# The keys of a paged cache brought in by blocks of 32 keys into all 128 partitions instead of by 256-column slices into 32 partitions

## The reference, cut to what matters

```python
def diff_attn_cached(q, k, v, kp, vp, lam):
    s_p = jnp.einsum('bqhd,bkhd->bhqk', q, kp).astype(F32) * scale
    s_n = jnp.einsum('bqhd,bkhd->bhqk', q, k).astype(F32) * scale
    ...
    a = _diff_combine(jnp.concatenate([s_p, s_n], axis=-1), lam)   # softmax, then map 0 - lam * map 1
    return (jnp.einsum('bhqk,bkhe->bqhe', a[..., :P], vp.astype(F32))
            + jnp.einsum('bhqk,bkhe->bqhe', a[..., P:], v.astype(F32)))

kp = cache_k[o][page_table].reshape(Bs, past, 2 * H_C, HD_C)       # cache_k (1, 320, 128, 16, 64)
vp = cache_v[o][page_table].reshape(Bs, past, H_C, 2 * HD_C)
```

## Time and profile before

| | |
|---|---|
| median of 3 runs | 2929.31 us (2927.39 to 2933.23) |
| the profiled execution's own time | 2932.32 us |
| its span, from the first to the last instruction | 2930.7 us |
| mean granted TensorE clock | 0.899 |
| TensorE, VectorE, ScalarE, GpSimd busy | 81%, 52%, 23%, 19% of the span |
| first key DMA issued, last key page turned | 1727.0 us, 2773.2 us |
| moved by DMAs in all | 536.70 MB |

### The profile page before, as it was taken

How to read it: one execution, slowest core, us unless ns; L and a number is a source line. 1 busy time by engine, 2 the same in 40 slices (tenths; PEclk the granted TensorE clock), 3 DMA queues, 4 the chain that set the end, 5 groups by cost and what they waited for, 6 DMA issues and landing times.

```text
span 2930.7 us, 44854 instructions
## 1 busy us (share of the span) xinstructions
PE 2387.4 (81%) x15136; PEld 1789.1 (61%) x15136; DVE 1523.6 (52%) x2401; ACT 670.7 (23%) x1767; POOL 543.7 (19%) x487
## 2 busy tenths in 40 slices
PE   8999999999859997999999983666657565656668
PEld 6889888988747774787888871322323232323347
DVE  5565643233246665324344326666667666657643
ACT  4122211111123333223111122222222122222221
POOL 4332432234000000002223200211111111111121
PEclk9999999999969999999999997878777777777779
DMA  5223322232177889223343349999999999999963
GB/s 168 80 81 102 104 84 78 80 118 81 65 188 235 272 273 298 89 86 104 94 127 92 110 130 254 294 282 288 289 276 289 263 267 277 280 267 274 276 196 115
DMA packets 443172, 536.70 MB, mean 183 GB/s; under 512 B 41365, under 2 KB 385314, under 8 KB 439754
## 3 DMA queue, kind: packets, MB, share of 16 engines
q1 hardware_dynamic: 404258, 395.54, 48.5%
q0 software_dynamic: 35712, 130.04, 14.6%
q10 hardware_dynamic: 3016, 8.82, 0.8%
HBM read 432.92 MB, written 101.22 MB: 182 GB/s over the span
## 4 chain that ended last, share of the span: by engine, by line
PE 56%; SPq 20%; DMA 10%; DVE 6%; issue 6%; ACT 1%; POOL 0%; POOLq 0%; ACTq 0%; DVEq 0%
SPq L2669 16%; DMA at_kp<-in_cache_k 8%; PE p_col L571 4%; PE p_col L573 4%; PE p_col L572 4%; PE p_gm L2274 4%; PE p_gm L2276 4%; PE p_gm L2275 4%; PE p_row L612 4%; PE p_row L614 3%; PE p_row L613 3%; SPq L2659 3%; PE oa_out L1832 2%; PE oa_out L1834 2%; PE oa_out L1833 2%
## 5 line engine op out<-in xcount | busy, mean ns | idle before, releaser
L3044 DVE STREAM_TRANSPOSE at_kT<-at_kp 128x1024 f32<-128x1024 f32 x256 | 315.3, 1240 | 280.0 <-DMA at_kp<-in_cache_k 263.3
L2832 PE MATMUL at_ssc<-at_kT,at_qz 128*32 128x256 f32 x2048 | 177.1, 505 | 224.8 <-DVE at_kT L3044 168.7
L2679 POOL DMA_DIRECT2D at_vp<-in_cache_v x248 | 132.6, 535 | 932.0 <-issue 925.7
L2832 PEld LDWEIGHTS at_ssc<-at_kT,at_qz 128*32 128x32 f32 x2048 | 77.5, 138 | 340.4 <-DVE at_kT L3044 210.3
L571 PE MATMUL p_col<-h_hi,p_wqk 128*128 128x352 f32 x768 | 251.3, 327 | 1.1 <-DVEq L800 1.1
L573 PE MATMUL p_col<-h_hi,p_wqk 128*128 128x352 f32 x768 | 247.1, 322 | 0.0
L572 PE MATMUL p_col<-h_lo,p_wqk 128*128 128x352 f32 x768 | 246.9, 321 | 0.0
L612 PE MATMUL p_row<-p_wvz,h_hi 128*128 128x512 f32 x512 | 203.7, 398 | 3.5 <-ACT p_vst L695 3.5
L2274 PE MATMUL p_gm<-p_whl,h_hi 128*128 128x512 f32 x512 | 203.1, 397 | 0.9 <-DVE h_lo L2411 0.6
L614 PE MATMUL p_row<-p_wvz,h_lo 128*128 128x512 f32 x512 | 202.0, 394 | 0.0
L613 PE MATMUL p_row<-p_wvz,h_hi 128*128 128x512 f32 x512 | 201.2, 393 | 0.0
(11 more groups left out here) (409 smaller groups left out, 4624.4 us busy)
## 6 DMA issues: line engine op xcount, KB each, us to landing
at_kp<-in_cache_k SPq DMA_DIRECT2D x1024, 128.0 KB, 8.1
at_vp<-in_cache_v POOLq DMA_DIRECT2D x248, 512.0 KB, 9.4
s_qk<-p_res SPq DMA_DIRECT2D x32, 528.0 KB, 2.8
p_wst<-in_w_in_a SPq DMA_DIRECT2D x32, 512.0 KB, 4.0
p_wst<-in_w_in_a SPq DMA_DIRECT2D x64, 256.0 KB, 2.9
mx_qk<-s_qk SPq DMA_DIRECT2D x16, 1024.0 KB, 9.2
p_wst<-in_w_in_c SPq DMA_DIRECT2D x64, 256.0 KB, 4.6
s_v<-p_vst SPq DMA_DIRECT2D x64, 128.0 KB, 2.9
```

Source lines behind the costliest of these rows:

```text
L2832: last = pe.matmul(ssc[at:at + 32, 0:2 * PAGE], qz[:, n // NGB, e, x // 2, x % 2, :], keys, start=x == 0, stop=x == 3)
L3044: dve.transpose(kT[:, n % 2, k, :], kp[n % 2][k][:]).then_inc(keys_turned, 1)
```

## The change

A page still comes with four DMAs of 128 KB into the same places of `kp`, and every contiguous piece is still 1024 B. What each DMA takes is different. Before, a DMA took one slice `x` of 256 columns of all 128 keys. After, it takes one block `y` of 32 keys with all their columns, and writes a column range of 256 numbers in all 128 partitions. The access pattern on the side of HBM had the 32 keys `i` outermost (32 x 4 pieces); now it has the four slices `x` outermost (4 x 32 pieces). On the side of SBUF it had 32 partitions outermost; now it has 128.

```diff
-            rows = g["cache_k"][0, bass.ds(number, 1)].rearrange("a (y i) h d -> i (a y) (h d)", i=32)
-            for x in range(4):
-                part = slice(32 * x, 32 * x + 32)
-                sp.dma_start(kp[n % 2][k][part, :].rearrange("i (y c) -> i y c", y=KB), rows[:, :, 256 * x:256 * x + 256]).then_inc(
-                    k_loaded[n % 2 * GP + k], 16)
+            rows = g["cache_k"][0, bass.ds(number, 1)].rearrange("a (y i) (x h) d -> (a y) x i (h d)", i=32, x=4)
+            for y in range(KB):
+                sp.dma_start(kp[n % 2][k][:, 256 * y:256 * y + 256], rows[y]).then_inc(k_loaded[n % 2 * GP + k], 16)
```

## The result

The changed kernel takes 3710.34 us (median of 4 runs, 3705.93 to 3714.64) against 2931.27 us before: 1.265 times as long, 95% interval 1.262 to 1.269. The forecast was 3995 us within 3700 to 4650. Direction and mechanism were right; the time lies only 10 us above the lower end of the range.

What follows compares the result with a forecast made beforehand. Full DMA engines bound the 1046 us key stretch. On four engines keys 1737, values 400 and rest 80 make 2217 us, over 1.05 2111 us, 1065 more than before: 3995 us predicted, range 3700 to 4650.

Steps and rivals of the forecast that it cites:

- Direction: Whole kernel: slower, given a chance of 0.92, against faster 0.05 and same 0.03.
- mechanism: Key DMAs: dealt to the same 4 engines, not 16; keys 1737 us on each at 53 ns per packet; chance 0.70.

Runs made afterwards that it cites:

- experiment 10: Kernel after, with GpSimd issuing the keys of groups 7 to 63 and SP the values from group 2 on; 5968 us, 2.039 of before.
- experiment 4: Kernel after, but each key DMA takes 128 rows of 1024 B, outermost 128 in HBM and SBUF; 2718 us, 0.927 of before.
- experiment 5: Kernel before, same slices and order in HBM, but each DMA written into a column range of all 128 partitions; 2870 us, 0.981 of before.
- experiment 6: Kernel before, but pieces in HBM ordered as 128 rows of 1024 B each, still written into 32 partitions; 2967 us, 1.015 of before.
- experiment 8: Kernel before, but each key DMA writes 64 partitions, outermost 64 on both sides; 2961 us, 1.011 of before.
- experiment 1: Kernel after, but each block of 32 keys comes with two DMAs of 64 KB, each with two slices outermost; 5073 us.
- experiment 2: Kernel after, but from group 2 on a value DMA brings 8 numbers per row instead of 1024; 3374 us.

## Why the prediction was right, and what was mis-sized

## What to carry to other kernels

Before changing the shape of a DMA, count on how many engines both sides let it be dealt: in all cases here the outermost count of each side decided, not the number of pieces (128 pieces went to 16 engines before and to 4 in the kernel after). On SP's and ScalarE's queues the counts of 4 B in the queue's row tell the number afterwards: 16, 4 or 2 per DMA on q1, 4 on q10. On GpSimd's queue every DMA seen left 16, experiment 10's with 4 outermost too, so there they can't be read this way without a further test. Then look at how many partitions a DMA writes, 71 to 73 ns per piece for 32 or 64 here and 47 to 50 for 128; where a layout forces 32 partitions per DMA, let successive DMAs alternate between partitions 0 to 63 and 64 to 127, which gave 1.6% here for a change of order. A queue that keeps its engines full may carry something dearer than it has to, as here 71 ns for a piece that can cost 47: compare the time of a packet with the same size elsewhere in the trace.

## What the runs showed of the hardware that was not expected

- SP's shortest issue of a key DMA of 128 KB depends on its shape: 316 ns before (and 332 in experiment 4), 537 to 564 in the kernel after and in experiments 5, 6 and 8. What in the shape decides is not settled; equal outermost counts don't (experiment 8 has 64 and 64).
- A packet of 1024 B costs 47 ns where four engines carry the keys, at 160 GB/s in all, and 47 to 48 where 16 engines write each DMA into 128 partitions, at 360. It costs 71 to 73 ns where each DMA of 16 engines writes into 32 or 64 neighbouring partitions (68 to 69 over the whole stage), at 253 to 274 GB/s.
- The packet times of a full engine add up to more than the time that passed: to 108 to 110% on the two or four engines that carry the keys in the kernel after and in experiments 1 and 2. With 16 engines full it was 105% in the kernel before, and 101% in experiment 4 from 2000 to 2040 us, at the same 47 ns. So the low price by itself doesn't bring the larger overlap; what does stays open.
